# Stick-breaking attention: logs in two rounded parts, and the mask added by TensorE

## The reference, cut to what matters

```python
z = jnp.einsum('bhtd,bhsd->bhts', qb, kb) * scale
strict = s_idx < t_idx
log_1m = jnp.where(strict, jax.nn.log_sigmoid(-z), 0.0)
suffix = lax.cumsum(log_1m, axis=3, reverse=True) - log_1m
a = jnp.where(strict, jnp.exp(jax.nn.log_sigmoid(z) + suffix), 0.0)
outs.append(jnp.einsum('bhts,bhsd->bhtd', a, vb))
```

## Time and profile before

| | us |
|---|---|
| median of 3 runs | 1706.14 (1705.45 to 1708.61) |
| the profiled execution, its own time | 1704.38 |
| its span in the trace | 1702.6 |
| TensorE busy | 1659.8 (97%) |
| VectorE busy | 1163.1 (68%) |
| ScalarE busy | 947.6 (56%) |
| GpSimd busy | 331.3 (19%) |
| granted TensorE clock, mean | 0.995 of full |

### The profile page before, as it was taken

How to read it: one execution, slowest core, us unless ns; L and a number is a source line. 1 busy time by engine, 2 the same in 40 slices (tenths; PEclk the granted TensorE clock), 3 DMA queues, 4 the chain that set the end, 5 groups by cost and what they waited for, 6 DMA issues and landing times.

```text
span 1702.6 us, 32619 instructions
## 1 busy us (share of the span) xinstructions
PE 1659.8 (97%) x13184; PEld 1600.8 (94%) x13184; DVE 1163.1 (68%) x1966; ACT 947.6 (56%) x1717; POOL 331.3 (19%) x307
## 2 busy tenths in 40 slices
PE   7999999999998999999999999999999999999997
PEld 6998989999997889999999999999999999999997
DVE  7899887555577865556676656766686756576666
ACT  6677765544455756444666545544465655454443
POOL 0100011244332212444211101001241111000025
PEclk9999999999999999999999999999999999999999
DMA  6433334555542256556535535556563444345663
GB/s 202 135 120 106 123 112 138 164 174 182 174 124 80 83 158 189 186 185 188 161 121 164 174 100 168 172 179 181 176 191 125 127 149 134 124 136 168 186 182 110
DMA packets 76326, 257.53 MB, mean 151 GB/s; under 512 B 8465, under 2 KB 12561, under 8 KB 75921
## 3 DMA queue, kind: packets, MB, share of 16 engines
q1 hardware_dynamic: 76176, 255.45, 48.4%
HBM read 254.37 MB, written 1.05 MB: 150 GB/s over the span
## 4 chain that ended last, share of the span: by engine, by line
PE 80%; DVE 10%; ACT 6%; issue 3%; POOL 0%; DMA 0%; POOLq 0%; DVEq 0%; SPq 0%; ACTq 0%
PE pb L142 79%; DVE WL L161 3%; DVE TMP L173 2%; ACT SCR L151 2%; DVE SCR L173 2%; ACT L158 1%; ACT WH L151 1%; PE pb L145 1%; DVE SCR L161 1%; ACT ASH L151 1%; ACT TMP L151 1%; ACT SCR L152 0%; ACT Rbuf L151 0%; DVE ASL L173 0%; ACT SQ L151 0%
## 5 line engine op out<-in xcount | busy, mean ns | idle before, releaser
L161 DVE TENSOR_TENSOR WL<-RAW,WH 128x1024 fp32r<-128x1024 f32 (+4 forms) x514 | 607.7, 1184 | 14.7 <-ACT WH L151 14.5
L142 PE MATMUL pb<-HNH,WH 128*128 128x256 f32 (+1 forms) x2056 | 596.3, 290 | 6.3 <-issue 2.4
L151 ACT ACTIVATE WH<-RAW 128x1024 fp32r<-128x1024 f32 (+4 forms) x514 | 506.9, 989 | 146.0 <-PE pb L142 142.7
L142 PE MATMUL pb<-HNH,WL 128*128 128x256 f32 (+1 forms) x2056 | 583.8, 284 | 0.0
L142 PE MATMUL pb<-HNL,WH 128*128 128x256 f32 (+1 forms) x2056 | 583.5, 284 | 0.0
L142 PE MATMUL pb<-ASH,WH 128*128 128x256 f32 (+1 forms) x1560 | 452.7, 290 | 5.9 <-DVE WL L161 2.7
L142 PE MATMUL pb<-ASH,WL 128*128 128x256 f32 (+1 forms) x1560 | 443.4, 284 | 0.0
L142 PE MATMUL pb<-ASL,WH 128*128 128x256 f32 (+1 forms) x1560 | 442.9, 284 | 0.0
L142 PEld LDWEIGHTS pb<-HNH,WH 128*128 128x128 f32 x2056 | 388.5, 189 | 13.8 <-issue 4.0
L142 PEld LDWEIGHTS pb<-HNH,WL 128*128 128x128 f32 x2056 | 389.1, 189 | 0.0
L142 PEld LDWEIGHTS pb<-HNL,WH 128*128 128x128 f32 x2056 | 387.4, 188 | 1.3
(11 more groups left out here) (158 smaller groups left out, 1738.8 us busy)
## 6 DMA issues: line engine op xcount, KB each, us to landing
RAW<-in_w_gu SPq DMA_DIRECT2D x88, 512.0 KB, 3.7
RAW<-in_w_up SPq DMA_DIRECT2D x64, 512.0 KB, 3.6
RAW<-in_w_down SPq DMA_DIRECT2D x64, 512.0 KB, 3.5
RAW<-in_w_ssd SPq DMA_DIRECT2D x48, 512.0 KB, 3.5
RAW<-in_w_xkv SPq DMA_DIRECT2D x32, 512.0 KB, 4.2
RAW<-in_w_mlin SPq DMA_DIRECT2D x24, 512.0 KB, 3.6
RAW<-in_w_fd SPq DMA_DIRECT2D x32, 384.0 KB, 3.0
RAW<-in_w_sbqkv SPq DMA_DIRECT2D x24, 512.0 KB, 4.1
```

The costliest lines, as they stand in the source:

```text
L142: return self.eng.matmul(o, l, r, start=start, stop=stop, skip_group_check=skip) if self.eng else Nothing()
L151: return self.eng.activation(o, i, f, bias=bias, scale=scale)
L161: return self.eng.tensor_tensor(o, a, b, op) if self.eng else Nothing()
```

## The change

Three things change in the stage.

1. **The mask goes to TensorE.** The product of the identity IDR with a mask of 0 and -1e30 (CMR, one 128-column block used twice) is added to both diagonal blocks of each head, behind the scores of both heads. Masked scores give L = 0 by themselves and a weight of 0. So the multiplication on GpSimd and the masking addition on VectorE go, and ScalarE's last Exp reads the bank and writes Ws.
2. **The suffix sums get rounded operands.** L is split in LH (a copy by ScalarE) and LL (L - LH, by VectorE), and ntge and nones are rounded once into SUF. Per head there are four products: SUF[0] with 384 columns and SUF[1] with 128, for LH and then for LL.
3. **The order.** ScalarE copies LH of both heads at k = 0, behind both Ln. VectorE makes LL at k = 1, behind its split and eviction of that step. At the start of the stage ScalarE rounds SUF and CMR.

The constants s384 and n384 (768 columns) give way to smask (128). The core of the diff:

```diff
             elif k == 2:
                 for e in range(2):
-                    z, L = banks[3 + e], Ls[:, s, e, :]
-                    q.wait_ge(*lm[c, e])
-                    q.matmul(z[:, 0:256], cc("ntge"), L[:, 0:256], False, False, True)
-                    q.matmul(z[:, 256:384], cc("ntge"), L[:, 256:384], False, True, True)
-                    q.matmul(z[:, 128:256], cc("nones"), L[:, 256:384], False, True, True).then_inc(*zs(c, e))
+                    z = banks[3 + e]
+                    q.wait_ge(*lhi[c, e])
+                    q.wait_ge(*llo[c, e])
+                    for L in (LH[:, s, e, :], LL[:, s, e, :]):
+                        q.matmul(z[:, 0:384], SUF[:, 0, :], L, False, False, True)
+                        t = q.matmul(z[:, 128:256], SUF[:, 1, :], L[:, 256:384], False, True, True)
+                    t.then_inc(*zs(c, e))
...
-                    q.matmul(z[:, 256:384], key[:, 128:256], qry[:, 128:256], False, False, True).then_inc(*zq(c, e))
+                    q.matmul(z[:, 256:384], key[:, 128:256], qry[:, 128:256], False, False, True)
+                q.wait_ge(*sufr["mask"])
+                for e in range(2):
+                    d = banks[3 + e][:, :].rearrange("p (a k) -> p a k", a=2)[:, :, 0:128]
+                    q.matmul(d, IDR[:, :], bc(CMR[:, :], 2), False, False, True).then_inc(*zq(c, e))
...
+                for e in range(2):
+                    q.wait_ge(*lsp[c, e])
+                    if c > 1:
+                        q.wait_ge(*zs[c - 2, e])
+                    q.activation(LH[:, s, e, :], Ls[:, s, e, :], ACT.Copy).then_inc(*lhi(c, e))
...
-            elif k == 2:
+            elif k == 1:
                 for e in range(2):
-                    q.wait_ge(*zs[c, e])
+                    q.wait_ge(*lhi[c, e])
                     if c > 1:
-                        q.wait_ge(*sbo[c - 2, e])
-                    q.tt(Ws[:, s, e, :], banks[3 + e][:, 0:384], cc("n384"), ALU.add).then_inc(*zd(c, e))
+                        q.wait_ge(*zs[c - 2, e])
+                    q.tt(LL[:, s, e, :], Ls[:, s, e, :], LH[:, s, e, :].bitcast(F32), ALU.subtract).then_inc(*llo(c, e))
...
         def act_sb(q):
             q.table(LOGS)
+            q.activation(SUF[:, 0, :], cc("ntge"), ACT.Copy)
+            q.activation(SUF[:, 1, :], cc("nones"), ACT.Copy)
+            q.activation(CMR[:, :], cc("smask"), ACT.Copy).then_inc(*sufr("mask"))
...
         def pool_sb(q):
-            for n in range(28):
-                for c, k in sb_cores(n):
-                    if k == 0:
-                        for e in range(2):
-                            L = Ls[:, c % 2, e, :]
-                            q.wait_ge(*lsp[c, e])
-                            q.tt(L, L, cc("s384"), ALU.mult).then_inc(*lm(c, e))
             pool_post(q, "sbo")
```

More of the change, by code:

```diff
@@ L25 @@
                ("ntge", 128), ("nones", 128),
[1 row of a table removed]
+               ("m384", 384), ("smask", 128), ("cmask", 128), ("sel2", 142), ("bdm", 128),
                ("i384", 1), ("i256", 1), ("rsel", 16), ("cs", 272), ("onerow", 256),
@@ L1886, in v_free @@
                     ("xkv1", 8): [xex[0, 3, 1]], ("xkv1", 9): [eva[AT["xkv0", 0, 13]]],
-                    ("xkv1", 14): [zd[7, 0]], ("xkv1", 15): [zd[7, 1]]}[name, m]
+                    ("xkv1", 14): [wex[7, 0]], ("xkv1", 15): [wex[7, 1]]}[name, m]
         def pe_post(q, post, ax, free, begun=()):
@@ L2646, in build_program @@
         Ls = carve(2, 2, 384)
+        LH = sb("LH", [128, 2, 2, 384], F32R)
+        LL = sb("LL", [128, 2, 2, 384], F32R)
+        SUF = sb("SUF", [128, 2, 128], F32R)
         Ws = carve(2, 2, 384)
         vtt, vtd = sig("sb_v_transposed"), sig("sb_v_copied")
-        zq, zs, zd = sig("z_ps"), sig("z_suffix_ps"), sig("z_masked")
-        la, lx_, ll, lsp, lm = sig("l_abs"), sig("l_exp"), sig("l_ln"), sig("l_softplus"), sig("l_masked")
+        zq, zs = sig("z_ps"), sig("z_suffix_ps")
+        la, lx_, ll, lsp = sig("l_abs"), sig("l_exp"), sig("l_ln"), sig("l_softplus")
+        lhi, llo, sufr = sig("l_high"), sig("l_low"), sig("suffix_operands")
         wex, sbo = sig("w_exp"), sig("sb_out_ps")
         def sb_cores(n):
-            return [(c, n - 3 * c - 3) for c in range(8) if n - 3 * c - 3 in (0, 2, 3)]
+            return [(c, n - 3 * c - 3) for c in range(8) if n - 3 * c - 3 in (0, 1, 2, 3)]
         def pe_sb_core(q, c, k):
@@ L2669, in pe_sb_core @@
                     if c:
-                        q.wait_ge(*zd[c - 1, e])
+                        q.wait_ge(*wex[c - 1, e])
                     else:
@@ L2717, in act_sb_core @@
                     if c > 1:
-                        q.wait_ge(*zs[c - 2, e])
+                        q.wait_ge(*llo[c - 2, e])
                     q.activation(L, z, ACT.Abs).then_inc(*la(c, e))
@@ L2723, in act_sb_core @@
                     q.activation(L, L, ACT.Ln, 1.0, cc("one")).then_inc(*ll(c, e))
+                for e in range(2):
[3 more added lines that the diff above has]
+                    q.activation(LH[:, s, e, :], Ls[:, s, e, :], ACT.Copy).then_inc(*lhi(c, e))
             elif k == 2:
                 for e in range(2):
[L2726 to L2729, removed]
+                    q.wait_ge(*zs[c, e])
+                    if c > 1:
+                        q.wait_ge(*sbo[c - 2, e])
+                    q.activation(Ws[:, s, e, :], banks[3 + e][:, 0:384], ACT.Exp).then_inc(*wex(c, e))
+            elif k == 3:
                 act_part(q, "sb", c, ASH[:, c, 0:T2], banks[6][:, 0:T2], use[AT["fd0_5", 0, 7]], sbo[c, 1])
@@ L2761, in dve_sb_core @@
                     q.stt(L, banks[3 + e][:, 0:384], 0.0, L, ALU.max, ALU.add).then_inc(*lsp(c, e))
-            elif k == 2:
+            elif k == 1:
                 for e in range(2):
-                    q.wait_ge(*zs[c, e])
+                    q.wait_ge(*lhi[c, e])
                     if c > 1:
-                        q.wait_ge(*sbo[c - 2, e])
-                    q.tt(Ws[:, s, e, :], banks[3 + e][:, 0:384], cc("n384"), ALU.add).then_inc(*zd(c, e))
-            else:
+                        q.wait_ge(*zs[c - 2, e])
+                    q.tt(LL[:, s, e, :], Ls[:, s, e, :], LH[:, s, e, :].bitcast(F32), ALU.subtract).then_inc(*llo(c, e))
+            elif k == 3:
                 dve_part(q, "sb", c, ASL[:, c, 0:T2], banks[6][:, 0:T2], ASH[:, c, 0:T2])
@@ L3001 @@
     put("m384", np.concatenate([le, one, le], 1))
-    put("s384", np.concatenate([lt, one, lt], 1))
-    neg = np.where(lt > 0, 0.0, -1e30).astype(np.float32)
-    put("n384", np.concatenate([neg, 0 * one, neg], 1))
+    put("smask", np.where(lt > 0, 0.0, -1e30).astype(np.float32))
     put("cmask", np.where(j[None, :] <= j[:, None], 0.0, -1e30).astype(np.float32))
```

2 lines of the change are left out of this document (1 added, 1 removed), and 1 row of the table _at.

## The result

The changed kernel takes 1708.76 us (median of 20 runs, 1707.11 to 1711.89), the kernel before 1705.44 us in the 20 runs beside them (1703.74 to 1708.61). The ratio is 1.0021, with a 95% interval of 1.0014 to 1.0027: slower by 3.3 us in the medians. The prediction was 1709.5 us, +3.4 us.

What follows compares the result with a forecast made beforehand. TensorE, busy for 97% of the span, was taken to bound the kernel; four ordinary cores at 0.0, three memory cores at +1.32 and the last at -0.6 made +3.4 us on 1706.14, so 1709.5 us, range 1704.8 to 1713.0.

Steps and rivals of the forecast that it cites:

- TensorE's own work: Per core on TensorE: suffix sums -1.76 us, eight rounded products +1.15, masks +0.24; -0.37 us, -3.0 over eight cores.
- the price of 0.111: Suffix sums: a rounded 128-column product loading its own weights costs 0.111 us, read from earlier trace rows.
- The masks' 0.24 us: TensorE, per core: two mask products of 256 rounded columns at 0.118 us each add 0.24 us.
- Abs 0.32 us late behind the mask: ScalarE's Abs waits for scores signalled behind the mask, starting at 1302.33 instead of 1302.01; everything behind moves by 0.32 us.
- The ordinary cores: Cores 0, 1, 2, 6: TensorE waits 0.37 us for the first head's LL, cancelling -0.37; net 0.0 us.
- The memory cores: Cores 3, 4, 5: ASL, waiting for ScalarE's memory copy ASH, delays LL; TensorE waits 1.69 us, net +1.32 each.
- The last core: Core 7: no wait for LL, masking adds gone, Exp held by ScalarE's weight copies; -0.6 us, 0.5 allowed either way.
- The sum: Whole kernel: 4 x 0.0 + 3 x 1.32 - 0.6 = +3.4 us.
- Costed at nothing: Start copies (0.9 us if uncovered), smaller constants transfer (at most 2 us gain), ScalarE's 16 added copies, Exp from PSUM: nothing.
- The gain did not survive: Rival: all waits for LL vanish in the stage, TensorE's gain survives; -3.2 us, 1702.9 us; 12 in 100.
- The memory cores did not wait as briefly as the ordinary ones: Rival: memory cores wait only as briefly as ordinary cores, ASH being taken earlier; -0.6 us, 1705.5 us; 13 in 100.
- the clock did not fall in the stage: Rival: 1.69 us waits drop TensorE's clock to half, 1.7 us per fall; one to three make 1711.2 to 1714.6; 15 in 100.

Runs made afterwards that it cites:

- ll_early: Changed kernel with VectorE's LL moved from k = 1 to k = 0, right behind the two maxima; 1702.15 us, ratio 0.9981 to the kernel before.
- no_ones: ll_early without its four 128-column products with SUF[1] per core, leaving out part of the sum; 1700.89 us, ratio 0.9973 to the kernel before.
- mask_only: Changed kernel with the mask on TensorE but fp32 suffix sums as before, no LH, LL or SUF; 1708.12 us, ratio 1.0012 to the kernel before.
- mem_first: Changed kernel with ScalarE's memory chunk copy (ASH) of steps 12, 15 and 18 ahead of the LH copies; 1706.80 us, ratio 1.0002 to the kernel before.
- split_only: Changed kernel with masks left on GpSimd and VectorE, suffix sums from LH and LL; 1721.34 us, ratio 1.0087 to the kernel before.
- ll_late: Changed kernel with VectorE's LL one step later, at k = 2; 1729.74 us, ratio 1.0145 to the kernel before.
- pool_ll: Changed kernel with LL computed by GpSimd instead of VectorE; 1715.19 us, ratio 1.0058 to the kernel before.
- split_early: split_only with VectorE's LL moved right behind the two maxima; 1713.19 us, ratio 1.0044 to the kernel before.

## Why the prediction was right

*TensorE's own work: -0.37 us per core.* Right, shown by ll_early, where nothing waits: 12.12 us against 12.50, with 1.15 us for the suffix sums and 0.11 for a 128-column product (no_ones). The trace sided with the price of 0.111 read from the earlier trace rows, not with the 81 ns of the Trainium skill (TensorE: Matmul & The Clock Gate, Back-to-back issue gap). The sum of 1.15 us shows it best; the core times of no_ones, at 0.09 each, lie between the two. The masks' 0.24 us were shown by mask_only.

*Abs 0.32 us late behind the mask.* Abs starts 1.58 us behind the transposes in core 1 of the changed kernel (1302.23 and 1300.65), 1.25 in the one before (1302.01 and 1300.76): 0.33.

*The ordinary cores: a wait of 0.37, net 0.0.* The wait is 0.38, the net +0.07: behind the wait the suffix sums take 1.22 us for my 1.15. I had priced them as they run with nothing to wait for.

*The memory cores: a wait of 1.69, net +1.32.* The wait is 1.70, the net +1.37. Each link stood where the queues put it: LH at 1331.28 for 1331.25, ASH 1331.71 for 1331.67, ASL 1332.14 for 1332.11, TensorE 1334.65 for 1334.62. One step was right without its reason: the weight split ahead of LL had 2.05 us in this core before, beside GpSimd's product (1331.13), and my step of 1.13 came from an ordinary core's 1.22. It fits because GpSimd leaves the stage, which the prediction counted only for a split behind LL. That 0.97 of the wait is the ASH link, mem_first showed; that all of it is LL's place in the queue, ll_early.

*The last core: -0.6.* From the transposes to the first product of the next block it was 10.84 us and is 10.06: -0.78. The two weight copies were late as counted (1388.71 behind transposes at 1382.79 is 5.92; before, 1383.02 behind 1378.57 was 4.45, so 1.47 for my 1.46), and Exp followed in the stead of VectorE's adds.

*The sum: +3.4.* Measured 3.44 in the trace and 3.3 in the medians. The mechanism is right, but that the sum is right to 0.1 us is in part luck. The ordinary cores came to +0.29 in all where I had 0, the memory cores to +4.10 for 3.96, and against these stand the last core's -0.78 for -0.6 and the 0.17 that the changed kernel was ahead when the stage began. The 0.7 us by which 1709.5 is too high lie in the base: the kernel before took 1706.14 us in the three runs that I added to and 1705.44 in the twenty beside the changed one.

*Costed at nothing.* The start copies cost nothing: the chain's first 104 products of the stage take 13.75 us in both traces. The smaller transfer gave at most the 0.17 us; the two executions had their clock falls ahead of the stage in the same places, so they can be compared.

*The rivals.* The gain did not survive, since ASL does hold LL up (ll_early shows what it would have been: 1702.15 for my 1702.9). The memory cores did not wait as briefly as the ordinary ones; mem_first is nearly that case, with a memory wait of 0.5 us, and by its ratio stands at +0.3 us where the rival had -0.6, with three memory waits that were 0.35 longer than its ordinary ones (0.53 and 0.18 to 0.20 in the view). In the profiled execution the clock did not fall in the stage; for the other nineteen no trace shows it. The rival's mechanism is real, at 1.5 us a fall for my 1.7. It came behind waits of 2.5 and 3.3 us (split_only, ll_late), behind one of four waits of 1.8 (ll_late's core 6), and twice behind two shorter ones close together (pool_ll). So that the 1.7 us of the changed kernel came without it is not shown to be more than luck, and how near they are to a fall stays open.

What I had chosen wrongly stands in the expectations, not in the forecast: the masks ahead of the scores as free, GpSimd as a helper at its undisturbed speed, and VectorE's weight split as never the limit.

## What to carry to other kernels

When a product is replaced by cheaper ones that need a new operand, count the saving on the bound engine first, then write down the clock time at which the new operand is ready and what stands ahead of it in its own engine's queue: here 3 us of saving and 6.6 us of waits hung on one line's place. An instruction that waits for another engine (ASL for ASH) delays everything queued behind it, so an addition to one engine's queue (LH) can surface two engines further on. When two engines share the work of moving data, price the second with the first running beside it, as the rows of a busy stretch have it.

## What the runs showed of the hardware

GpSimd and VectorE take turns when both work on two operands in SBUF, as the rows of this case show it: of two instructions that overlap, the one that came first keeps its length, and the other gets longer by about what was left of the first. In split_early GpSimd's product started at 1309.40 and kept its 1.02 us; VectorE's LL, started 0.02 later, took 1.41, and so ended 0.41 behind GpSimd's end. In the kernel before, VectorE's first weight split was there first and kept its 1.22 us, while GpSimd's product took 1.93 instead of 1.02; the second split then met the rest of that product and took 1.71. That 1.22 is thus no row of VectorE alone, but it is also what the split takes with GpSimd idle (1332.48 in the changed kernel). In pool_ll a subtraction of 384 columns took GpSimd 2.0 us with VectorE splitting weights and 1.0 with VectorE waiting, and VectorE's ASL behind the latter took 1.28 us instead of 0.42. An eviction, which reads one of its operands from PSUM, kept its 0.42 us beside GpSimd (pool_ll, 1310.70). So taking GpSimd out of the stage made VectorE faster: behind the place of LL in ordinary cores, but ahead of it in memory cores.

The length of one wait does not tell whether the granted clock falls. It fell to half behind all three TensorE waits of 3.3 us (ll_late), but behind only two of three waits of 2.5 us in memory cores (split_only; not behind the one that ended at 1354.96), one of four waits of 1.8 us (ll_late), and none of the changed kernel's three of 1.7. And in pool_ll it fell behind two waits of 0.3 and 1.2 us, one after the other, in cores 0 and 7, while the same pair in cores 1, 2 and 6 came without a fall. Three of pool_ll's windows, columns as above:

```profile
1295.20:1298.60 3.40, 1.95 (x14) 1.60 (x13) 3.33 (x5) 1.84 (x3) 2.83 (x2) 1.00 0.67 167
1298.60:1302.00 3.40, 3.40 (x18) 3.40 (x17) 0.52 (x1) 1.44 (x2) 0.00 (x0) 0.50 0.73 242
1302.00:1305.40 3.40, 3.40 (x30) 2.64 (x29) 1.13 (x3) 0.38 (x1) 0.00 (x0) 1.00 0.15 58
```

TensorE was busy for 1.95 of 3.40 us ahead of this fall, for 2.12 with no fall in the changed kernel's window at 1331.00, and for 1.57 with no fall in ll_late's at 1294.00. So the busy time of a stretch that I cut out doesn't tell it either. Nor does the program alone. Ahead of the stage all kernels that descend from the changed one do the same work, and still in mem_first's execution the clock was at 0.69 of full from 241.40 to 244.80, where in the changed kernel's it was at 1.00, with TensorE busy for 2.29 and 2.31 us of the 3.40 before. mem_first's first transposes of the stage stand at 1291.60, those of the changed kernel at 1288.07. So one execution without a fall does not show that a wait is harmless; what decides it was not found. A fall lasted 3.4 us here and in ll_late, and 6.8 for the first and the last of split_only; one of 3.4 us cost 1.5 us in each of these three kernels (pool_ll's core 0 took 15.50 us, its ordinary cores 1 and 2 14.0).
